# One matrix product for both token tiles in a gated scan, and a key block moved behind the spatial gating

## What is computed

```python
def hgrn2(h, w_in, w_out, lower_bound, onorm_g):        # layer 1: the scan, 8 heads of 128
    q, f, i, g = jnp.split(h @ w_in, 4, axis=-1)
    log_f = ...                                          # gate of every token and channel
    key = 1.0 - jnp.exp(log_f)
    qf, vf = silu(q), i
    # per head: o[t] = sum over s <= t of (sum over k of qf[t,k] key[s,k] exp(G[t,k]-G[s,k])) vf[s]
    # where G is the running sum of log_f over the tokens
    o = rmsnorm(o, onorm_g).reshape(B, S, D_MODEL) * jax.nn.silu(g)
    return o @ w_out

def chunked_sgu(h, w_in, w_out, vnorm_g, w_s, b_s):     # layer 2: the spatial gating
    u, v = jnp.split(jax.nn.gelu(h @ w_in, approximate=False), 2, axis=-1)
    v = rmsnorm(v, vnorm_g)
    mixed = (w_s * tril) applied along 128 tokens of v, by group, + b_s
    return (u * mixed) @ w_out
```

## Time and profile before

| | us |
|---|---|
| median of 3 runs | 2531.73 |
| lowest and highest | 2530.61, 2533.63 |
| the profiled execution, whole | 2536.24 |
| its span | 2534.4 |
| PE busy in the span | 2469.9 |
| DVE busy | 1311.8 |
| ACT busy | 1087.3 |

### The profile page before, as it was taken

How to read it: one execution, slowest core, us unless ns; L and a number is a source line. 1 busy time by engine, 2 the same in 40 slices (tenths; PEclk the granted TensorE clock), 3 DMA queues, 4 the chain that set the end, 5 groups by cost and what they waited for, 6 DMA issues and landing times.

```text
span 2534.4 us, 32787 instructions
## 1 busy us (share of the span) xinstructions
PE 2469.9 (97%) x11808; PEld 1842.2 (73%) x11808; DVE 1311.8 (52%) x1912; ACT 1087.3 (43%) x1640; POOL 82.9 (3%) x126
## 2 busy tenths in 40 slices
PE   9999998999998999999999999999999999999998
PEld 7876433676442677888888888888788888778887
DVE  5644111554121676555557656555555555765554
ACT  4553111452110564454455455445455444644543
POOL 0000000100000100000000100000000000000000
PEclk9999999999999999999999999999999999999999
DMA  6548999748999735465452255555455564353652
GB/s 233 201 154 323 378 409 409 255 163 337 392 409 409 255 121 172 132 230 184 164 174 100 93 165 191 194 181 172 166 162 191 187 198 158 117 183 127 222 197 101
DMA packets 149951, 545.59 MB, mean 215 GB/s; under 512 B 17064, under 2 KB 17265, under 8 KB 149834
## 3 DMA queue, kind: packets, MB, share of 16 engines
q1 hardware_dynamic: 144522, 525.52, 58.4%
q0 software_dynamic: 5024, 17.43, 2.0%
q10 hardware_dynamic: 288, 1.05, 0.1%
HBM read 542.87 MB, written 2.63 MB: 215 GB/s over the span
## 4 chain that ended last, share of the span: by engine, by line
PE 57%; DVE 5%; ACT 2%; issue 2%; POOL 0%; POOLq 0%; ACTq 0%; DVEq 0%
PE bank L2416 17%; PE bank L2418 17%; PE bank L2417 17%; DVE low_w L1393 2%; PE bank L2497 2%; PE bank L3134 1%; ACT tmp L1170 1%; ACT high_w L886 1%; PE bank L2988 1%; PE bank L2846 1%; PE bank L3021 1%; DVE proj L2029 0%; DVE tmp L2047 0%; POOL stat L766 0%; DVE table L2071 0%
## 5 line engine op out<-in xcount | busy, mean ns | idle before, releaser
L2416 PE MATMUL bank<-high_w,xh 128*128 128x512 f32 x2112 | 842.3, 399 | 8.9 <-DVE low_w L1393 3.1
L1393 DVE TENSOR_TENSOR low_w<-stage_w,high_w 128x1024 fp32r<-128x1024 f32 x528 | 641.6, 1223 | 383.1 <-ACT high_w L886 355.4
L2418 PE MATMUL bank<-high_w,xl 128*128 128x512 f32 x2112 | 825.5, 391 | 0.0
L2417 PE MATMUL bank<-low_w,xh 128*128 128x512 f32 x2112 | 824.6, 390 | 0.0
L886 ACT ACTIVATE high_w<-stage_w 128x1024 fp32r<-128x1024 f32 x528 | 554.0, 1058 | 192.3 <-PE bank L2418 188.8
L2416 PEld LDWEIGHTS bank<-high_w,xh 128*128 128x128 f32 x2112 | 397.9, 188 | 100.5 <-issue 11.6
L2418 PEld LDWEIGHTS bank<-high_w,xl 128*128 128x128 f32 x2112 | 397.6, 188 | 85.0
L2417 PEld LDWEIGHTS bank<-low_w,xh 128*128 128x128 f32 x2112 | 398.1, 188 | 77.7
L1805 DVE TENSOR_TENSOR qk<-qk,bank 128x256 f32<-128x256 f32 x32 | 13.5, 421 | 230.2 <-ACT qk L1055 230.2
L2416 PE MATMUL bank<-high_d,hidden_h 128*128 128x512 f32 x320 | 124.9, 390 | 0.0
L1892 DVE TENSOR_TENSOR hidden_l<-bank,hidden_h 128x512 fp32r<-128x512 f32 x40 | 27.7, 692 | 187.5 <-ACT hidden_h L1126 187.5
(11 more groups left out here) (348 smaller groups left out, 2788.6 us busy)
## 6 DMA issues: line engine op xcount, KB each, us to landing
stage_w<-in_wide SPq DMA_DIRECT2D x592, 512.0 KB, 4.4
pair_w<-in_wide SPq DMA_DIRECT2D x128, 512.0 KB, 13.9
stage_d<-in_down SPq DMA_DIRECT2D x120, 512.0 KB, 4.3
proj<-in_wide SPq DMA_DIRECT2D x64, 512.0 KB, 12.4
pair_d<-in_down SPq DMA_DIRECT2D x64, 512.0 KB, 15.0
proj<-in_down SPq DMA_DIRECT2D x32, 512.0 KB, 13.7
gain<-in_gains POOLq DMA_DIRECT2D x18, 512.0 KB, 5.2
skew<-bias_dram POOLq DMA_DIRECT2D x1, 1536.0 KB, 16.3
```

Source lines behind the costliest of these rows:

```text
L1393: vec.tensor_tensor(low_w[:, w], stage_w[:, w], high_w[:, w].bitcast(F32), ALU.subtract)\
L2416: pe.matmul(o, hi, wh, start=start, stop=False)
L2417: pe.matmul(o, hi, wl, start=False, stop=False)
L2418: return pe.matmul(o, lo, wh, start=False, stop=stop)
```

## The change

**Scan.** One product now serves both token tiles of a head. Of the two operands, `fixed` holds tile 0's keys in the first halves and tile 1's queries in the second halves, `moving` holds tile 0's queries in the second halves and tile 1's keys in the first halves. Tile 0's part of the result lies in the columns of the second halves, as before; tile 1's part lies in the columns of the first halves, and is transposed. So `scaled` has four products of 256 columns where there were two of 512, and `merge` copies 256 columns for each tile. Masks are transposed at the start (PE, seven transposes; ACT, two copies), and tile 1's matrices at the end (`turn_blocks`; ACT copies them, `keep_turned`). Exponentials alternate between `y` and `plain_x1` (`decays`), banks between 4, 5 and 6, 7 (`hg_bank`). DVE's order within a step, PE's order at the end of the scan and ACT's order of taking the results change too. `plain_x0` and `plain_x1` lie over `xh` and `xl`.

**Gating.** In layer 2 the key block goes from ahead of the norm's transposes to behind the spatial gating; PE's products go into banks 6, 7, 2 and 3, one token tile after the other, without the wait for `taken`.

```diff
@@ plan @@
-        if layer == 2:
-            first_keys(2048, 6)
...
             add("sgu", mixed=2)
+            first_keys(2048, 2)
             turn("y", "s", hook=True)
@@ ACT, hgrn @@
+                act.wait_ge(hg_out, 1)
+                act.activation(turned_masks(0, 4), bank[6][:, :], ACT.Copy)
+                act.activation(turned_masks(4, 7), bank[7][:, 0:3 * P], ACT.Copy).then_inc(hg_spans, 1)
                 for k in range(HG_LEVELS + 1):
                     for b in range(4):
                         act.wait_ge(hg_sums, 4 * k + b + 1)
-                        if k:
-                            act.wait_ge(hg_x, 2 * k)
-                        act.activation(y[:, b * 512:(b + 1) * 512], bank[b][:, :], ACT.Exp).then_inc(hg_decay, 1)
+                        if k >= 2:
+                            act.wait_ge(hg_x, 2 * k - 2)
+                        act.activation(decays(k)[:, b * 512:(b + 1) * 512], bank[b][:, :], ACT.Exp).then_inc(hg_decay, 1)
...
+                act.wait_ge(hg_out, 2)
+                keep_turned(0)
+                act.wait_ge(hg_x, 2 * HG_LEVELS + 2)
+                act.wait_ge(hg_out, 3)
+                keep_rows(0)
+                act.wait_ge(hg_out, 4)
+                keep_rows(2)
+                act.wait_ge(hg_out, 5)
+                keep_turned(1)
+                act.wait_ge(hg_out, 6)
+                keep_rows(1)
+                act.wait_ge(hg_out, 7)
+                keep_rows(3)
@@ DVE, hgrn @@
+                def scaled(k, w):
+                    side, lv = k % 2, hg_level(k, w)
+                    if k:
+                        dve.wait_ge(hg_prod, hg_made(k - 1, w))
...
+                    for out, t, rows, second in ((fixed, 0, ks, 0), (fixed, 1, qs, 1), (moving, 0, qs, 1), (moving, 1, ks, 0)):
+                        ins = vec.tensor_tensor(halves(out, lv, second), halves(e[:, t], lv, second),
+                                                halves(rows[:, t], lv, second), ALU.mult)
+                    ins.then_inc(hg_x, 1)
+                def merge(k, w):
+                    side, lv = k % 2, hg_level(k, w)
+                    made = bank[hg_bank(k, w)]
+                    dve.wait_ge(hg_prod, hg_made(k, w))
...
+                    for t, mask in enumerate((proj[:, MASK0 + lv * P:MASK0 + (lv + 1) * P], turned_masks(lv, lv + 1))):
+                        dve.wait_ge(hg_kept, hg_merged(k, w) - 3 + t)
+                        one = halves(mask.bitcast(U32).rearrange("p (j m) -> p j m", j=1), lv, 1 - t)
+                        vec.copy_predicated(halves(blocks_of(side)[:, :, t, :], lv, 1 - t),
+                                            one.broadcast_to([P, 4, P >> (lv + 1), 1 << lv]),
+                                            halves(made[:, :].rearrange("p (j m) -> p j m", j=4), lv, 1 - t)).then_inc(hg_kept, 1)
                 for k in range(HG_LEVELS + 1):
                     dve.wait_ge(hg_decay, 4 * (k + 1))
+                    scaled(k, 0)
+                    if k:
+                        merge(k - 1, 1)
+                    scaled(k, 1)
+                    merge(k, 0)
+                merge(HG_LEVELS, 1)
@@ PE, hgrn: products @@
+                        pe.wait_ge(hg_kept, hg_merged(k - 2, w) if k >= 2 else 2 * k + w + 1)
+                        for j in range(4):
+                            at = w * D + j * P
+                            mm = pe.matmul(bank[hg_bank(k, w)][:, j * P:(j + 1) * P], tmp[:, at:at + P],
+                                           tmp[:, at + 512:at + 512 + P], start=True, stop=True)
+                        mm.then_inc(hg_prod, 1)
@@ PE, hgrn: order @@
-                for k in range(HG_LEVELS + 1):
-                    if k < HG_LEVELS:
-                        sums(k + 1)
+                for k in range(HG_LEVELS):
+                    sums(k + 1)
                     products(k)
+                pe.wait_ge(hg_decay, 4 * (HG_LEVELS + 1))
+                pe.wait_ge(hg_kept, hg_merged(HG_LEVELS - 1, 1))
+                turn_blocks(0)
+                outputs(0, range(0, 4))
+                products(HG_LEVELS)
+                pe.wait_ge(hg_spans, 4)
+                outputs(1, range(0, 4))
+                pe.wait_ge(hg_kept, hg_merged(HG_LEVELS, 1))
+                turn_blocks(1)
+                outputs(0, range(4, 8))
+                pe.wait_ge(hg_spans, 5)
+                outputs(1, range(4, 8))
@@ PE, sgu @@
                 pe.wait_ge(sg_w_ready, 1)
-                pe.wait_ge(taken[0], s.out)
-                pe.wait_ge(taken[1], s.out)
-                for grp in range(8):
-                    for t in range(T):
+                for t in range(T):
+                    for grp in range(8):
```

More of the change, by code:

```diff
@@ L539, in spans, with hg_level, hg_made, hg_merged @@
             return (hidden_l if pair >= 2 else hidden_h)[:, pair % 2 * 2 * P:(pair % 2 + 1) * 2 * P]
-        def hg_made(k, v):
-            if k < 6:
-                return 4 + 4 * k + 2 * (v + 1)
-            return 28 + 3 * (k - 6) + 2 + v
+        def hg_level(k, w):
+            return k // 2 * 2 + w
+        def hg_made(k, w):
+            return 4 + 2 * k + w + 1
+        def hg_merged(k, w):
+            n = 4 + sum(1 if hg_level(q, v) == HG_LEVELS else 2 for q in range(k) for v in range(2))
+            return n + (2 if w == 0 else 3 if hg_level(k, w) == HG_LEVELS else 4)
+        def hg_bank(k, w):
+            return 4 + 2 * (k % 2) + w
+        def decays(k):
+            return plain_x[1][:, 0:2 * D] if k % 2 else y[:, :]
+        def turned_masks(a, b):
+            return plain_x[0][:, (2 + a) * P:(2 + b) * P]
+        def turned_blocks(side):
+            return pair_d[1][:, side * 512:(side + 1) * 512]
+        def blocks_of(side):
+            return proj[:, side * 4096:side * 4096 + D].rearrange("p (j t m) -> p j t m", j=4, t=T)
+        def halves(a, lv, second):
+            return a.rearrange("p j (c b l) -> p j c b l", b=2, l=1 << lv)[:, :, :, second]
         def columns(s, i):
@@ L2178, in norm_heads @@
                 for t in range(T):
[L2179 removed]
+                    dve.wait_ge(hg_taken, t + 3)
                     rstd(HEADS0 + 8 * t, 8, P)
@@ L3089, in hgrn @@
                 v = pv(4096)
+                pe.wait_ge(table_in, 48)
+                for lv in range(HG_LEVELS):
+                    mm = pe.transpose(bank[6 + lv // 4][:, (lv % 4) * P:(lv % 4 + 1) * P],
+                                      proj[:, MASK0 + lv * P:MASK0 + (lv + 1) * P], ident[:, :])
+                mm.then_inc(hg_out, 1)
                 for t in range(T):
@@ L3159, in sgu @@
                 pe.wait_ge(sg_w_ready, 1)
-                pe.wait_ge(taken[0], s.out)
-                pe.wait_ge(taken[1], s.out)
-                for grp in range(8):
-                    for t in range(T):
-                        mm = pe.matmul(bank[4 + grp // 2][:, (grp % 2) * S + t * P:(grp % 2) * S + (t + 1) * P],
+                for t in range(T):
+                    for grp in range(8):
+                        mm = pe.matmul(sgu_bank(t, grp)[:, (grp % 4) * P:(grp % 4 + 1) * P],
                                        proj[:, 4096 + grp * P:4096 + (grp + 1) * P],
```

111 lines of the change are left out of this document (39 added, 72 removed).

## The result

| | before | changed |
|---|---|---|
| median, us | 2531.17 (4 runs) | 2517.07 (4 runs) |
| lowest and highest | 2530.52, 2533.63 | 2516.21, 2517.62 |
| span of the profiled execution | 2534.4 | 2514.4 |

The changed kernel takes 0.9942 of the time of before, with a 95% interval of 0.9926 to 0.9958: 14.1 us less by the medians, 10.6 to 18.7 by the interval. Forecast were 2517.7 us and 14.0 us less. In a second comparison (run e4) the ratio was 0.9941 (0.9926 to 0.9955).

A forecast was written before the change was run, and what follows sets the result against it. PE, busy in 97% of the span, bounds the kernel. Steps -10.0, end of the scan +1.0 and gating -5.0 make -14.0 us, from the median 2531.7 to 2517.7 us; range 2514.0 to 2524.5.

The forecast's parts named there:

- The bound: Scan steps: halved products leave PE 4.05 us a step, DVE needs 4.32 and becomes the bound.
- third rival: Scan steps: the second buffer brings no overlap, a step keeps 5.84 us; 2527.7 us in all; chance 5%.
- The size of DVE's work: Scan, DVE's first product of first step to that of last: 30.0 us with overlapped operations, saving 10.0.
- first rival: Scan: DVE pays each record in full, -4.6 us in the steps, +1.4 at the end; 2523.5 us; chance 14%.
- The opening: Scan start: mask transposes fit PE's old wait (0 to 0.1 us), ACT's mask copies are covered; cost 0.
- The end of the scan: From DVE's first product of the last step to the key block: 13.1 us against 12.07, 1.0 lost.
- The term for the clock: End of the scan: lower PE clock behind the 1.9 us wait, as in the kernel before, costs 1.6 us.
- the other branch: End of the scan if PE's clock holds: 11.5 us, a gain of 0.6.
- The gating: Layer 2 gating: 3.5 us of PE waits and 1.7 of lower clock go, less 0.2: 5.0 saved.
- my 0.2 for changes between groups: Gating: 0.2 us taken off the saving for PE's changes between groups.
- The sum: Whole kernel: -10.0 + 1.0 - 5.0 = -14.0 us, from the median 2531.7 to 2517.7.
- The slower rival: Scan steps: PE's clock falls to its lower level for good; +12.7 us, 2544.4 us; chance 4%.

The follow-up runs named there:

- e4: The changed kernel measured again, against the kernel before: median 2518.31 us, ratio 0.9941.
- e5: The changed kernel with one buffer for the exponentials instead of two; ratio to before 0.9991.
- e1: The changed scan with the gating and the key block of before; median 2520.07 us, ratio to before 0.9949.
- e7: The changed kernel with mask halves of levels 0 and 1 copied side by side by ACT; DVE's first product of first step to that of last 29.56 us.
- e8: The changed kernel with the last step's first products ahead of PE's block transposes and ACT's second turned blocks ahead of the rows; ratio to before 0.9936.
- e9: The changed kernel, masked copies of levels 0 and 1 reading the bank side by side; DVE's first product of first step to that of last 29.57 us.
- e11: The changed kernel with the last step's first products ahead of PE's block transposes, ACT's order unchanged; ratio to before 0.9942.
- e10: The changed kernel, masked copies of levels 0 and 1 writing the target side by side; DVE's first product of first step to that of last 27.82 us.
- e3: The kernel before with only the gating's banks, order and removed wait changed, key block at its old place; ratio to before 0.9998.
- e2: The scan of before with the changed gating and the key block behind it; median 2527.28 us, ratio to before 0.9979.
- e6: The changed kernel with masked copies of all 512 columns for each tile; ratio to before 0.9967.

## Why the prediction was right

**The bound.** PE with 4.05 us a step and DVE with 4.3: PE's step measured 4.01, a higher-level step took 4.02 or 4.15, with DVE busy without gaps and PE waiting 0.2 us or less in it. Right, but by less than forecast: there the two engines are level. The ring of waits that would have kept 5.84 us (third rival) is real, as e5 shows, and it is the second buffer that opens it.

**The size of DVE's work.** Forecast 30.0 us for the seven steps, measured 29.54 to 29.58 in seven profiles (the changed kernel, e1, e4, e7, e8, e9, e11). Within it two errors cancel, which is luck: I took 0.40 us for every masked copy. Eighteen of them took 0.34 (1.1 us less) and eight 0.51 to 0.58 (1.2 us more). I had written that strided masks were not in the trace; what I didn't see was that the target's runs were the open point. The first rival (records paid in full, 5.3 us a step) fell: four products in a row took 1.34 to 1.38 us, not 1.7. The Trainium skill's formula, page "VectorE: DVE Perf Modes", section "The TRN2 errata — SBUF-src ops pay a fixed extra latency per instruction", gives the record (0.42 us) and not the step from start to start.

**The opening.** PE's mask transposes and ACT's copies were forecast at nothing. From the group of transposes ahead of the scan to DVE's first product it is 31.0 us in both kernels. The timeline of the changed kernel shows the transposes in the old wait, and 0.16 us of it left:

```profile
1354.06 0.93 PE L3148 MATMUL bank<-ident,proj 128*128 128x128 f32 x7
...
1355.14 0.36 PE L3167 MATMUL bank<-hidden_h,high_d 128*128 128x256 f32 x1 [0.16 <-issue]
```

**The end of the scan.** This is the step that failed: forecast 1.0 us lost, measured 0.8 us gained (11.27 us against 12.07). The order of the waits and their sizes were right (1.9 and 1 us forecast, 1.69 and 0.87 measured). The term for the clock, 1.6 us, was wrong in this execution and in all six profiles with this wait (the changed kernel, e1, e4, e7, e9, e10): the products behind it run at full clock. I had concluded from two falls to a rule; the other branch, 11.5 us if the clock holds, is what came. Against an execution of before without a fall (e3, 10.45 us from its last step's first product at 1401.17 to its key block at 1411.62, or 1.6 under 12.07) the new end is 0.8 us longer, for the transposes and the wait for ACT. So at full clock in both the term is 0.8 us of loss, near the forecast 1.0; what was wrong was to put the same clock into both executions. The one of before had the fall (1.6 us), the one of the changed kernel had none.

**The gating.** Forecast 5.0, measured 5.7 in the trace and 5.3 by time (3.0 to 7.6). The three waits have gone (3.5 us), the lower clock too (1.7); my 0.2 for changes between groups was not needed, and 0.5 us more came, whose place the record doesn't show. The 1.7 us was no sure part of the gain: e3 has the same wait and no fall, and from e3 to the changed kernel the stretch gives 3.6 us. At equal clock e2 is 3.6 us faster. The free place of the key block ahead of the norm cost nothing, as the scan layer had shown: there is the same wait of 0.24 us inside the last down product and none behind it. That the wait for `taken` is worth nothing by itself (e3) doesn't touch the sum, but I had counted it as 0.96 us of its own; it is only so with the key block behind.

**The sum.** The gain was under-forecast by 1.8 us at the end of the scan, 0.7 in the gating and 0.4 in the steps, so the traces show 16.9 us for 14.0. The medians show 14.1 and 14.3. Most of the difference is the clock. Without the two falls in the profile of before (1.6 and 1.7 us) the traces give 13.6, and the executions at equal clock give 13.4. The rest fits that executions of before have the lower clock a little more often (0.9949 on average against 0.9954, some 0.9 us by the line above). So the sum at full clock is -10.4 + 0.8 - 4.0 = -13.6. That 14.0 met 14.1 so closely is in part luck: a fall that I counted as a sure gain in the gating (1.7 us) is one only in some executions, and the steps gave a little more.

**The slower rival.** PE kept its clock in the steps of the changed kernel, with waits of 0.2 to 1.0 us in four of the seven steps, and in those of e6, with one of 1.0 to 1.2 us in each from the second on. The rival's cause is real all the same. In e5, behind a wait of 0.56 and one of 1.30 us in the same step, the clock fell once in the steps; eight products took 1.90 us in place of 1.16 (timeline of PE, then busy time by stretch):

```profile
1377.80 1.90 PE L3190 MATMUL bank<-tmp 128*128 128x128 f32 x8 [1.30 <-DVE tmp L2304]
```

```profile
1379.00:1380.00 1.00, 1.00 (x7) 1.00 (x6) 0.06 (x1) 0.91 (x2) 0.00 (x0) 0.50 0.00 0
```

The clock was back at 1.00 from 1382 us on, and the step of DVE from 1379.94 still took 5.62 us, like the next ones, since PE had room there. The Trainium skill tells of a clock that swings with short idles (page "TensorE: Matmul & The Clock Gate", section "A second HAM failure mode: psum-queue depth-cycling"). No profile here shows it swing from step to step; e5 shows one such fall.

## What to carry to other kernels

Where an engine's work is halved, look first at the ring that ties it to the others: here the halved products gave 0.5 us until ACT had a second buffer (39.5 us before it, 29.6 with it), and the next engine in line (DVE) was the bound at once. A filler block paid here behind the stage whose successor waits for a chain of small steps on other engines, and what its old place costs without it was read at a twin that already goes without it. A term that rests on the clock of the matrix engine is a chance, not a price: give it both values in the sum, and compare executions at equal granted clock too.

## What the hardware showed that I had not expected

**Falls of the clock after a wait.** The same wait in the same instructions is followed by 1.2 GHz in one execution and not in the next. Each row of the table is one wait of PE, by the profile in which it stands:

| wait | length, us | clock fell behind it | clock held |
|---|---|---|---|
| ahead of transposes in the differential attention, around 956 us, the same in all kernels | 1.79 to 1.86 | before, e2, e5 | the ten others |
| before the last products, scan of before | 1.98 to 1.99 | before, e2 | e3 |
| ahead of the output block, gating of before | 1.77 to 1.86 | before, e1 | e3 |
| ahead of the block transposes | 1.69 | none | changed kernel, e1, e4, e7, e9, e10 |
| the same with full columns | 2.09 | e6 | |
| the same with one buffer | 3.15 | e5 | |
| in a step with one buffer | 1.30 | e5, once | e5, once |

Busy time by stretch behind the waits of 2.09 and 3.15 us, of e6 and of e5 (columns as in the earlier trace rows; the granted clock, 0.50 and 0.67, is the number after POOL's):

```profile
1401.00:1404.00 3.00, 2.89 (x14) 2.92 (x15) 1.16 (x2) 0.60 (x2) 0.00 (x0) 0.50 0.00 0
```

```profile
1404.00:1408.00 4.00, 3.53 (x21) 3.56 (x22) 1.53 (x3) 2.02 (x10) 0.00 (x0) 0.67 0.02 4
```

Where PE was the bound a fall cost 1.3 to 1.7 us (4.27 and 4.57 us for products that take 2.94; 1.6 in e5), and in e6, where the lower clock lasted longer (0.51 still from 1404 to 1407 us), 2.8 us. The same wait ahead of the same transposes was followed by a fall in three of thirteen profiles.

**Masked copies into short runs.** A masked copy of 256 columns into runs of one or two elements costs 0.51 to 0.58 us from start to start, into longer runs 0.34. Mask and source may have short runs at no cost (e7, e9).

**Overlap on DVE.** Products and masked copies of 256 columns recorded with 0.42 to 0.44 us start 0.34 us apart, also across the change from one kind to the other.
